# Moving three kinds of VectorE subtractions to GpSimd, with a new order of plain and Winograd chunks, in a one-core encoder layer

## Chip, cores, metric

The kernel runs on one core of one Trainium2 chip. The metric is the device time of one execution in microseconds. Before the change three executions took 937.6, 938.48 and 938.74 us, so the median is 938.48 us.

## What is computed

One layer of a streaming encoder for 512 tokens of width 1024, in float32:

```
x = x + 0.5 * swiglu_ffn(rms_norm(x, ffn1_norm), ffn1_w_in, ffn1_w_out)
h = rms_norm(x, mix_norm); q, k, v, xr, gate = split(h @ w_in_proj)
x = x + concat([diff_attention(q, k, v, ...), rg_lru_branch(xr, gate, ...)]) @ w_out_proj
x = x + 0.5 * swiglu_ffn(rms_norm(x, ffn2_norm), ffn2_w_in, ffn2_w_out)

def swiglu_ffn(h, w_in, w_out):          # w_in: 1024 x 5632, w_out: 2816 x 1024
    g, u = split(h @ w_in)
    return (silu(g) * u) @ w_out
```

The change touches the two feed-forward blocks (FFN 1 and FFN 2).

## The kernel before

**Arithmetic.** Each float32 operand of a large matmul is split into a high part in fp32r (`w_hi`, `t_hi`, `act_hi`, made by ScalarE with a Copy that rounds) and a low part (`w_lo`, `t_lo`, `act_lo`, the difference, made by VectorE). A product is three matmuls, high by high, high by low and low by high (lines 1367 to 1369 in `product`). Everything is held transposed: features on the 128 partitions, 512 tokens along the free dimension.

**Chunks.** The work of an FFN is a list of chunks, one weight load of 640 to 1024 KB each, into two slots by parity (`raw`, `w_hi`, `w_lo`). The 22 tiles of the hidden dimension stand in two groups of 10 and 12. Each group's input chunks are followed by 8 output chunks ("O"). The first 4 input chunks of an FFN are plain ("P"): 8 steps of contraction for the gate and 8 for the up part, 512 columns wide, 48 matmuls. The others, 6 in the first group and 12 in the second, are Winograd-Strassen chunks ("W"): seven block products instead of eight, each of 4 steps, 3 matmuls and 256 columns, so 84 matmuls. The products are called op 0 to op 6.

**Operands of a W chunk.** For the moving side, x is combined once per FFN from blocks of pairs of feature tiles into T1 to T4 (`t_bases` on ScalarE, `t_made_of` on VectorE, T1 being a plain difference of two halves of x, line 864) and then split (`t_highs`, `t_lows`). For the weights, VectorE makes four sums per chunk (`s123`, `s4`), ScalarE rounds them (`s_highs`), VectorE takes their low parts (`s_lows`). The low parts of the unsummed blocks come from ScalarE writing minus the high part (`minus_highs`, line 521) and a GpSimd DMA that adds `raw` to it (`a_lows`, line 463).

**Results of a W chunk.** Op 0 gives Q6 and op 1 gives Q1. ScalarE copies both out of PSUM (`copies(c, 0)`, `copies(c, 1)`, line 544); op 3 accumulates into the bank that held Q6 and waits for the first copy. VectorE forms Q1 - Q6 (`take_q6`, line 911), Q5 (`take_q5`), the two halves of the up part (`up_earlier`, `up_later`) and of the gate (`gate_later`, `gate_earlier`, the latter ending in line 943); ScalarE applies silu (line 549); VectorE multiplies (`product`, line 959); ScalarE rounds the result (`act_highs`, line 554), VectorE takes its low part (`act_lows`, line 965).

**Order.** Nothing is scheduled automatically. Each engine's queue is written out by hand per chunk (`plain_step`, `wino_step`, `out_step`), and semaphores hold an instruction until what it needs is there. An engine executes its queue in order, so a waiting instruction holds all behind it. In ScalarE's `wino_step(c)` the order is: `minus_highs(c+1)`, `act_highs(c-1)`, `copies(c, 0)`, `s_highs(c+1, 0)`, `copies(c, 1)`, `a_highs(c+1)`, the other `s_highs(c+1)`, `silu(c)`. In the plain chunks PSUM banks alternate between two sets, so TensorE waits before chunk k (k of 2 and 3) for `prod_made` of chunk k-2. At the end of the squares VectorE computes the reciprocal of the root (`reciprocal_root`, line 848), and only then, in `plain_step`, the first T blocks and the first gate.

Of the kernel before, what the change touches and what calls it, by code (L numbers as in the profile page):

```python
# [28 lines left out]
F32 = mybir.dt.float32  # L29
# [7 lines left out]
P = 128  # L37
# [98 lines left out]
def build(nc, xT, pos, cols_in, rows_in, bd_in, w_in1, w_out1a, w_out1b, w_rnn, w_qkv, w_proj, w_in2, w_out2a, w_out2b, out):  # L136
    stack = ExitStack()
    with stack:
# [14 lines left out]
        rows = sb("rows", [P, 6 * MAP_DIM])  # L153
# [16 lines left out]
        x = region("x", [P, KT * SEQ], F32, tile_at(0))  # L170
        raw = region("raw", [P, 2 * SLOT], F32, tile_at(8))

        w_hi = region("w_hi", [P, 2 * SLOT], F32R, tile_at(16))
        ws_hi = region("ws_hi", [P, 2 * BLOCK], F32R, tile_at(24))
        ws_lo = region("ws_lo", [P, 2 * BLOCK], F32R, tile_at(26))
        w_lo = region("w_lo", [P, 2 * SLOT], F32R, tile_at(28))

        t_hi = region("t_hi", [P, 2 * KT * SEQ], F32R, tile_at(36))
        t_lo = region("t_lo", [P, 2 * KT * SEQ], F32R, tile_at(52))
        h_hi = region("h_hi", [P, KT * SEQ], F32R, tile_at(36))  # L180
        h_lo = region("h_lo", [P, KT * SEQ], F32R, tile_at(44))
        base = tile_at(52)
        act_at = 68
        act_hi = region("act_hi", [P, GROUP[1] * SEQ], F32R, tile_at(act_at))
        act_lo = [region(f"act_lo{g}", [P, GROUP[g] * SEQ], F32R, tile_at(act_at + (14, 12)[g])) for g in range(2)]
        pairbuf = [region(f"pairbuf{b}", [P, 4 * SEQ], F32, tile_at(act_at + (10, 6)[b])) for b in range(2)]
        sums = region("sums", [P, 4 * BLOCK], F32, tile_at(92))
        up_s = region("up_s", [P, 2 * SEQ], F32, tile_at(96))
        assert tile_at(98) <= nc.sbuf_usable_end, (tile_at(98), nc.sbuf_usable_end)
# [3 lines left out]
        at = base  # L193
        places = {}
        for name, size in (("gt", 4 * KB2), ("xc", 4 * KB2), ("ra", 4 * KB2), ("ib", 4 * KB2),
                           ("th", 4 * KB2), ("qn", 4 * KB2), ("kn", 4 * KB2), ("v", 4 * KB2), ("qT", 4 * KB2),
                           ("kT", 4 * KB2), ("a", 2 * KB2), ("aT", 2 * KB2), ("bd", 2 * KB2)):
            places[name] = at
            at += size
        assert at <= tile_at(98)  # L200
        at = tile_at(24)
        for name, size in (("xrp", 2 * XP * 4), ("mask", (P + 64) * 4), ("st", 128 * 4), ("decay", 2 * RT * 4),
                           ("map_gain", 8), ("eps_o", 4)):
            places[name] = at
            at += -(-size // 32) * 32
        assert at <= tile_at(28)
# [17 lines left out]
        map_gain = region("map_gain", [P, 2], F32, places["map_gain"])  # L224
        eps_o = region("eps_o", [P, 1], F32, places["eps_o"])
# [40 lines left out]
        op_done, copied, post, t_made = sem("op_done"), sem("copied"), sem("post"), sem("t_made")  # L266
        t_base, t_step, t_sums, t_high, t_low = (sem(n) for n in ("t_base", "t_step", "t_sums", "t_high", "t_low"))
# [42 lines left out]

        def s_place(op, s):
# [18 lines left out]
        q_parts = [[region(f"q_part{m}{n}", [P, HALF], F32, tile_at((36, 52)[m]) + n * 4 * KB2) for n in range(4)] for m in range(2)]  # L330
# [24 lines left out]

        def half(t, c, n):
            return t[:, c % 2 * SEQ + n * HALF:c % 2 * SEQ + (n + 1) * HALF]
# [17 lines left out]

        T_SUMS = ((0, 1), (2, 3), (), ())
        T_SPLIT = ((), (0, 1), (2, 3), ())
# [6 lines left out]
        def _(sp):  # L384
# [23 lines left out]
            def load_ffn(f, first):  # L408
                c = C_FFN[f]
                w_in, w_outs = ((w_in1, (w_out1a, w_out1b)), (w_in2, (w_out2a, w_out2b)))[f]  # L410
                for g in range(2):
# [3 lines left out]
                    for d in range(KT):  # L415
                        load(w_outs[g], d, c + OUT_AT[g] + d, OUT_COLS[g])
# [9 lines left out]
            sp.dma_start(rows[:, :], rows_in).then_inc(params_landed[1], 16)  # L426
# [16 lines left out]
        def _(pool):  # L443
# [21 lines left out]

            def ffn(f):
                for c in range(C_FFN[f], C_FFN[f] + FFN_CHUNKS):
                    if kind(c) == "W":
                        a_lows(c)
# [16 lines left out]
        def _(act):  # L486
# [82 lines left out]
            def plain_step(f, c):  # L569
                following = kind(c + 1)  # L570
                k = c - C_FFN[f]
                if following == "P" and k >= 2:
                    highs(c + 1, IN_COLS)
                if following == "W":
                    minus_highs(c + 1)
                    s_highs(c + 1, 0, c - 1)
                    a_highs(c + 1)
                    s_highs(c + 1, 2)
                    s_highs(c + 1, 3)
                for p in T_SPLIT[k]:  # L580
                    t_highs(f, p)
                for p in T_SUMS[k]:
                    t_bases(f, p)
                silu(f, c)
                if following == "W":
                    s_highs(c + 1, 5, c)
                act_highs(f, c)

            def wino_step(f, c):
                following = kind(c + 1)  # L590
                if following == "W":
# [9 lines left out]
                if following == "W":  # L601
# [7 lines left out]
            def out_step(f, c):  # L609
# [15 lines left out]
                if (f, g) == (0, 0) and d == 5:  # L625
# [11 lines left out]
            def ffn(f):  # L637
# [11 lines left out]
                if f == 0:  # L649
                    squares(EARLY_SQUARES, KT)  # L650
                    act.wait_ge(consts_made, CONSTS_FIRST)
                if kind(c0 + 2) == "P":
                    highs(c0 + 2, IN_COLS)
                root((1, 3)[f])
# [161 lines left out]
        def _(dve):  # L816
# [29 lines left out]
            def reciprocal_root(n):  # L846
# [3 lines left out]
                dve.memset(sq_sum[:, :], 0.0).then_inc(dve_step, 1)  # L850
                links[0] += 1
                dve.wait_ge(rstd_made, n)
                dve.wait_ge(dve_step, links[0])

            LATER, EARLIER = slice(HALF, SEQ), slice(0, HALF)

            def t_made_of(f, p):
# [3 lines left out]
                steps = 2 * (KT // 2 * f + p)  # L861
                if p >= 2:
                    dve.wait_ge(t_low, KT // 2 * f + p - 1)
                dve.tensor_tensor(t_block(p, T1), even[:, LATER], even[:, EARLIER], ALU.subtract).then_inc(t_step, 1)
                dve.wait_ge(t_base, KT // 2 * f + p + 1)
                dve.scalar_tensor_tensor(t_block(p, T3), even[:, EARLIER], g_even, t_block(p, B22), ALU.mult, ALU.subtract)
                dve.wait_ge(t_step, steps + 1)
                dve.scalar_tensor_tensor(t_block(p, T2), t_block(p, T1), g_even, t_block(p, B22), ALU.mult, ALU.add).then_inc(t_step, 1)
                dve.wait_ge(t_step, steps + 2)
# [36 lines left out]
            def take_q6(c):  # L906
                w = wino_of(c)
                dve.wait_ge(copied, 2 * w + 2)
                if w >= 2:
                    dve.wait_ge(post, 5 * w - 6)  # L910
                dve.tensor_tensor(q16(c), q1_copy(c), q6_copy(c), ALU.subtract).then_inc(t_made, 1)

            def take_q5(c):
                w = wino_of(c)
# [34 lines left out]
            def product(f, c):  # L949
# [4 lines left out]
                else:  # L954
# [3 lines left out]
                    up = bank[3 * (c % 2) + 1][:, :]  # L958
                dve.tensor_tensor(both(up_s, c), up, both(gate_s, c), ALU.mult).then_inc(prod_made, 1)  # L959

            def act_lows(f, c):
                n = tile_of(c - C_FFN[f])
                g = int(n >= GROUP[0])
                dve.wait_ge(act_high, FT * f + n + 1)
                dve.tensor_tensor(tile(act_lo[g], n - FIRST_TILE[g]), both(up_s, c), tile(act_hi, n - FIRST_TILE[g]).bitcast(F32),
                                  ALU.subtract).then_inc(act_low, 1)

            def plain_step(f, c):
                k = c - C_FFN[f]
                following = kind(c + 1)  # L970
                if following == "P" and k >= 2:
# [753 lines left out]
```

## Time and profile before

| | value |
|---|---|
| median of 3 runs | 938.48 us |
| profiled execution, its own time | 937.22 us |
| its span, first to last instruction | 935.4 us |
| mean granted TensorE clock | 0.996 |
| busy: TensorE matmul / weight load | 97% / 85% of the span |
| busy: VectorE / ScalarE / GpSimd | 72% / 51% / 4% |
| DMA | 117.69 MB, 126 GB/s on average |

A busy TensorE is not TensorE at its peak: matmuls are pipelined, so one that is shown as 0.28 us long starts 0.12 us after the one before it. The pace is read from the starts. The profile also gives, in brackets, how long an engine was idle ahead of an instruction and what released it.

### The profile page before, as it was taken

The page shows a single profiled execution, that of the slowest core. Times are in us where ns is not written, and L with a number is a line of the kernel's source. Part 1 is how long each engine was busy: PE and PEld are TensorE (multiplying, and loading weights), DVE is VectorE, ACT ScalarE, POOL GpSimd, SP SyncE. Part 2 cuts the span into 40 slices and gives each one's busy share as a digit, 9 for nine tenths or more (in the row PEclk, how much of TensorE's full clock was granted, in tenths as well). Part 3 has the DMA queues.
Part 4 walks back from the last instruction along what each step waited for, and adds up shares of the span by engine and source line. Part 5 has one row for each costly group of instructions (what it writes and reads, how often), then busy time and mean ns, then how long its engine had stood idle before and what let it go on. Part 6 is the DMA issues. An engine that isn't in the chain of part 4 may idle for free.

```text
span 935.4 us, 14482 instructions
## 1 busy us (share of the span) xinstructions
PE 905.8 (97%) x5450; PEld 797.3 (85%) x5450; DVE 669.1 (72%) x1196; ACT 474.6 (51%) x803; POOL 34.1 (4%) x61
## 2 busy tenths in 40 slices
PE   8889999999999999999997999989999999999998
PEld 7679988899999888777885778779988899999886
DVE  6878865688887575765879777778854688887442
ACT  7466622465664333356647654466622465665220
POOL 0000000000000000000000000000000000010000
PEclk9999999999999999999999999999999999999999
DMA  7147522566664234222221021247532676664340
GB/s 268 57 133 184 155 99 87 176 181 174 185 174 122 98 101 141 106 91 90 90 91 46 1 91 51 85 128 186 148 108 84 179 182 164 195 170 124 122 134 34
DMA packets 21500, 117.69 MB, mean 126 GB/s; under 512 B 2640, under 2 KB 2768, under 8 KB 14160
## 3 DMA queue, kind: packets, MB, share of 16 engines
q1 hardware_dynamic: 16128, 88.32, 27.1%
q0 software_dynamic: 5328, 28.84, 15.5%
q8 instruction: 21, 0.34, 0.1%
q14 instruction: 23, 0.19, 0.1%
HBM read 86.74 MB, written 2.10 MB: 95 GB/s over the span
## 4 chain that ended last, share of the span: by engine, by line
PE 53%; DVE 18%; ACT 16%; issue 11%; DMA 1%; SPq 0%; DVEq 0%; ACTq 0%
PE bank L1367 17%; PE bank L1369 16%; PE bank L1368 16%; ACT w_lo L521 4%; ACT w_hi L527 3%; DVE sums L892 3%; DVE ws_lo L904 2%; ACT ws_hi L538 2%; ACT act_hi L554 2%; ACT q_part L544 2%; DVE sq L943 1%; DVE up_s L929 1%; DVE sq L941 1%; DVE sq L935 1%; DVE w_lo L831 1%
## 5 line engine op out<-in xcount | busy, mean ns | idle before, releaser
L1367 PE MATMUL bank<-t_hi,w_hi 128*128 128x256 f32 (+1 forms) x848 | 256.7, 303 | 10.6 <-DVE up_s L959 5.4
L1368 PE MATMUL bank<-t_lo,w_hi 128*128 128x256 f32 (+1 forms) x848 | 254.7, 300 | 0.0
L1369 PE MATMUL bank<-t_hi,w_lo 128*128 128x256 f32 (+1 forms) x848 | 254.7, 300 | 0.0
L1367 PEld LDWEIGHTS bank<-t_hi,w_hi 128*128 128x128 f32 x848 | 163.0, 192 | 18.6 <-issue 7.8
L1368 PEld LDWEIGHTS bank<-t_lo,w_hi 128*128 128x128 f32 x848 | 163.2, 192 | 5.7 <-issue 0.5
L1369 PEld LDWEIGHTS bank<-t_hi,w_lo 128*128 128x128 f32 x848 | 163.0, 192 | 5.4
L501 ACT ACTIVATE w_hi<-raw 128x1024 fp32r<-128x1024 f32 (+2 forms) x106 | 89.0, 887 | 146.2 <-PE bank L1369 146.2
L1367 PE MATMUL bank<-act_hi,w_hi 128*128 128x512 f32 x352 | 137.0, 389 | 0.0
L1368 PE MATMUL bank<-act_lo,w_hi 128*128 128x512 f32 x352 | 137.0, 389 | 0.0
L1369 PE MATMUL bank<-act_hi,w_lo 128*128 128x512 f32 x352 | 136.9, 389 | 0.0
L831 DVE TENSOR_TENSOR w_lo<-raw,w_hi 128x1024 fp32r<-128x1024 f32 (+2 forms) x106 | 103.5, 1018 | 14.6 <-ACT w_hi L501 14.0
L1035 DVE SCALAR_TENSOR_TENSOR up_s<-bank,rstd 128x512 f32<-128x512 f32 x32 | 22.1, 690 | 103.9 <-PE bank L1369 103.9
L1367 PE MATMUL bank<-t_hi,ws_hi 128*128 128x256 f32 x288 | 84.4, 293 | 5.0 <-ACT q_part L544 3.5
L549 ACT ACTIVATE sq<-sq 128x512 f32<-128x512 f32 x44 | 27.8, 632 | 119.4 <-DVE sq L943 88.4
L1368 PE MATMUL bank<-t_lo,ws_hi 128*128 128x256 f32 x288 | 81.4, 283 | 0.0
L1369 PE MATMUL bank<-t_hi,ws_lo 128*128 128x256 f32 x288 | 81.3, 282 | 0.0
L1369 PEld LDWEIGHTS bank<-act_hi,w_lo 128*128 128x128 f32 x352 | 66.1, 188 | 13.8
L1367 PEld LDWEIGHTS bank<-act_hi,w_hi 128*128 128x128 f32 x352 | 66.1, 188 | 13.7
L1368 PEld LDWEIGHTS bank<-act_lo,w_hi 128*128 128x128 f32 x352 | 66.1, 188 | 13.4
L538 ACT ACTIVATE w_hi<-sums 128x512 fp32r<-128x512 f32 x72 | 45.1, 627 | 56.1 <-PE bank L1369 45.6
L904 DVE TENSOR_TENSOR w_lo<-sums,w_hi 128x512 fp32r<-128x512 f32 x72 | 49.6, 688 | 31.1 <-ACT w_hi L538 31.1
L1367 PEld LDWEIGHTS bank<-t_hi,ws_hi 128*128 128x128 f32 x288 | 55.0, 191 | 10.9 <-ACT q_part L544 7.1
(216 smaller groups left out, 1532.4 us busy)
## 6 DMA issues: line engine op xcount, KB each, us to landing
raw<-w_in_dram SPq DMA_DIRECT2D x43, 1024.0 KB, 4.8
w_lo<-raw POOLq DMA_DIRECT2D x36, 768.0 KB, 5.7
raw<-w_out1b_dram SPq DMA_DIRECT2D x8, 768.0 KB, 4.3
raw<-w_qkv_dram SPq DMA_DIRECT2D x6, 1024.0 KB, 4.8
raw<-w_out2b_dram SPq DMA_DIRECT2D x8, 768.0 KB, 4.4
raw<-w_out1a_dram SPq DMA_DIRECT2D x8, 640.0 KB, 3.8
raw<-w_out2a_dram SPq DMA_DIRECT2D x8, 640.0 KB, 3.8
raw<-w_rnn_dram SPq DMA_DIRECT2D x4, 1024.0 KB, 4.8
```

What stands on the lines that cost most here:

```text
L501: act.activation(w_hi[:, part], raw[:, part], ACT.Copy).then_inc(high_made, 1)
L521: act.activation(w_lo[:, at:at + A_COLS], raw[:, at:at + A_COLS], ACT.Copy, scale=-1.0).then_inc(minus_made, 1)
L527: act.activation(w_hi[:, part], raw[:, part], ACT.Copy).then_inc(high_made, 1)
L538: act.activation(hi[:, at:at + BLOCK], s_sum(op), ACT.Copy).then_inc(s_high, 1)
L549: act.activation(both(gate_s, c), both(gate_s, c), ACT.Silu).then_inc(silu_made, 1)
L831: dve.tensor_tensor(w_lo[:, part], raw[:, part], w_hi[:, part].bitcast(F32), ALU.subtract).then_inc(low_made, 1)
L892: dve.tensor_tensor(s_sum(0), s_sum(2), raw_block(c, 0), ALU.add).then_inc(s2_made, 1)
L904: dve.tensor_tensor(lo, s_sum(op), hi.bitcast(F32), ALU.subtract).then_inc(s_low, 1)
L1035: dve.scalar_tensor_tensor(both(up_s, c), bank[OUT_BANK + s][:, :], 0.5, rstd[:, :], ALU.mult, ALU.mult).then_inc(y_taken, 1)
L1367: pe.matmul(dst, s_hi, m_hi, start=first, stop=False, skip_group_check=added)
L1368: pe.matmul(dst, s_hi, m_lo, start=False, stop=False, skip_group_check=added)
L1369: return pe.matmul(dst, s_lo, m_hi, start=False, stop=last, skip_group_check=added)
```

## The change

1. A new map of SBUF. The weights come first, then the region of activations, then t_lo, t_hi, x and raw. The last four, and the `q_part` buffers in them, are shifted by 64 bytes (`T_SHIFT`). `rows` moves into a region that the summed weights use, so its load and what reads it come later (second output group of FFN 1).
2. GpSimd now makes T1 (`t_ones`), Q1 - Q6 (`take_q6`) and the low parts of the activations (`act_lows`). They stand in its queue with the DMA of `a_lows`.
3. In ScalarE's `wino_step(c)`: `copies(c, 0)`, `minus_highs(c+1)`, `copies(c, 1)`, `act_highs(c-1)`, `s_highs(c+1, 0)`, `a_highs(c+1)`, the other `s_highs`, `silu(c)`. In VectorE's, `s_lows(c+1, 0)` comes after `take_q5`, and `s_lows(c+1, 2)` and `(c+1, 3)` both come after `up_earlier`.
4. The four plain chunks have four pairs of PSUM banks, and TensorE no longer waits for `prod_made` between them. The first two T blocks are made before or around the reciprocal root, the weights of the fourth plain chunk are split a chunk earlier, and the sum of squares of FFN 2 is taken inside the first plain chunk.

```diff
-        T_SUMS = ((0, 1), (2, 3), (), ())
-        T_SPLIT = ((), (0, 1), (2, 3), ())
+        ACT_AT, T_LO_AT, T_HI_AT, X_AT, RAW_AT, T_SHIFT = 20, 50, 66, 82, 90, 64
+        t_lo = region("t_lo", [P, 2 * KT * SEQ], F32R, tile_at(T_LO_AT) + T_SHIFT)
+        t_hi = region("t_hi", [P, 2 * KT * SEQ], F32R, tile_at(T_HI_AT) + T_SHIFT)
+        PLAIN_BANKS = ((0, 1), (3, 4), (2, 7), (5, 6))
...
+            # GpSimd
+            def t_ones(f, p):
+                if f == 0:
+                    pool.wait_ge(x_landed[2 * p], 16)
+                else:
+                    pool.wait_ge(x_updated, X_UPDATED[1] + 2 * p + 1)
+                if p >= 2:
+                    pool.wait_ge(t_low, KT // 2 * f + p - 1)
+                even = tile(x, 2 * p)
+                pool.tensor_tensor(t_block(p, T1), even[:, LATER], even[:, EARLIER], ALU.subtract).then_inc(t_one, 1)
+            def take_q6(c):
+                w = wino_of(c)
+                pool.wait_ge(copied, 2 * w + 2)
+                if w >= 2:
+                    pool.wait_ge(post, 5 * w - 6)
+                pool.tensor_tensor(q16(c), q1_copy(c), q6_copy(c), ALU.subtract).then_inc(t_made, 1)
+            def act_lows(f, c):
+                n = tile_of(c - C_FFN[f])
+                g = int(n >= GROUP[0])
+                pool.wait_ge(act_high, FT * f + n + 1)
+                pool.tensor_tensor(tile(act_lo[g], n - FIRST_TILE[g]), both(up_s, c), tile(act_hi, n - FIRST_TILE[g]).bitcast(F32),
+                                   ALU.subtract).then_inc(act_low, 1)
+            def wino_step(f, c):
+                if kind(c + 1) == "W":
+                    a_lows(c + 1)
+                take_q6(c)
+                if kind(c - 1) != "O":
+                    act_lows(f, c - 1)
+                if kind(c + 1) == "O":
+                    act_lows(f, c)
...
             # ScalarE
             def wino_step(f, c):
                 following = kind(c + 1)
+                copies(c, 0)
                 if following == "W":
                     minus_highs(c + 1)
                 else:
                     highs(c + 1, OUT_COLS[c - C_FFN[f] >= IN_AT[1]])
-                if kind(c - 1) == "W":
+                copies(c, 1)
+                if kind(c - 1) != "O":
                     act_highs(f, c - 1)
-                copies(c, 0)
                 if following == "W":
                     s_highs(c + 1, 0)
-                copies(c, 1)
-                if following == "W":
                     a_highs(c + 1)
...
             # VectorE
             def wino_step(f, c):
                 following = kind(c + 1)
                 if following == "W":
                     s4(c + 1)
-                    s_lows(c + 1, 0)
-                if kind(c - 1) == "W":
-                    act_lows(f, c - 1)
-                take_q6(c)
                 take_q5(c)
                 if following == "W":
-                    s_lows(c + 1, 2)
+                    s_lows(c + 1, 0)
                 up_earlier(c)
                 if following == "W":
+                    s_lows(c + 1, 2)
                     s_lows(c + 1, 3)
...
+            def plain_step(f, c):
+                if k == 0:
+                    gate(f, c)
+                    t_lows(f, 0)
+                    product(f, c)
+                    t_lows(f, 1)
+                    lows(c + 3, IN_COLS)
+                if k == 1:
+                    gate(f, c)
+                    t_made_of(f, 2)
+                    product(f, c)
+                    t_made_of(f, 3)
+                    s123(first_wino)
+                if k == 2:
+                    gate(f, c)
+                    t_lows(f, 2)
+                    product(f, c)
+                    t_lows(f, 3)
+                    s4(first_wino)
+                    s_lows(first_wino, 0)
+                    s_lows(first_wino, 2)
+                    s_lows(first_wino, 3)
+                if k == 3:
+                    gate(f, c)
+                    product(f, c)
+                    s_lows(first_wino, 5)
+                    s123(first_wino + 1)
...
             # TensorE
             def plain(f, c, meanwhile=None):
-                k = c - C_FFN[f]
                 pe.wait_ge(low_made, lows_through(c))
-                if k >= 2:
-                    pe.wait_ge(prod_made, FT * f + k - 1)
```

## Rows read from the trace of the kernel before

**Rows 1.** The page, busy time of each engine over the span.
```profile
PE 905.8 (97%) x5450; PEld 797.3 (85%) x5450; DVE 669.1 (72%) x1196; ACT 474.6 (51%) x803; POOL 34.1 (4%) x61
```
**Rows 2.** Waits of TensorE: us in total, times, longest.
```profile
PE bank L1367 <- DVE up_s L959: 5.4, 2, 4.2
PE bank L1367 <- DVE w_lo L831: 4.5, 3, 2.5
PE bank L1367 <- ACT q_part L544: 3.5, 4, 1.8
```
**Rows 3.** Timeline of TensorE in W chunks: start, duration, line, operands.
```profile
215.50 0.39 PE L1367 MATMUL bank<-t_hi,ws_hi 128*128 128x256 f32 x1
...
224.24 0.28 PE L1367 MATMUL bank<-t_hi,ws_hi 128*128 128x256 f32 x1
...
225.56 0.28 PE L1369 MATMUL bank<-t_hi,ws_lo 128*128 128x256 f32 x1
225.89 0.38 PE L1367 MATMUL bank<-t_hi,ws_hi 128*128 128x256 f32 x1
```
**Rows 4.** Timeline of TensorE, third and fourth plain chunk of FFN 2.
```profile
598.11 0.47 PE L1367 MATMUL bank<-t_hi,w_hi 128*128 128x512 f32 x1 [1.19 <-DVE up_s L959]
...
608.88 0.39 PE L1369 MATMUL bank<-t_hi,w_lo 128*128 128x512 f32 x1
611.76 0.50 PE L1367 MATMUL bank<-t_hi,w_hi 128*128 128x512 f32 x1 [2.49 <-DVE w_lo L831]
```
**Rows 5.** Stretches after stalls: length, busy by engine, PEclk, DMA.
```profile
36.20:38.90 2.70, 2.70 (x6) 2.12 (x7) 1.70 (x3) 2.70 (x5) 0.00 (x0) 0.50 0.00 0
...
611.80:616.00 4.20, 4.20 (x12) 3.29 (x13) 3.50 (x6) 1.36 (x2) 0.00 (x0) 0.59 0.74 250
```
**Rows 6.** Timeline of ScalarE over one W chunk.
```profile
223.04 0.63 ACT L549 ACTIVATE sq<-sq 128x512 f32<-128x512 f32 x1 [2.23 <-DVE sq L943]
223.58 1.47 ACT L521 ACTIVATE w_lo<-raw 128x1536 fp32r<-128x1536 f32 x1
224.96 0.61 ACT L554 ACTIVATE act_hi<-up_s 128x512 fp32r<-128x512 f32 x1
225.48 0.36 ACT L544 ACTIVATE q_part<-bank 128x256 f32<-128x256 f32 x1
225.74 0.62 ACT L538 ACTIVATE w_hi<-sums 128x512 fp32r<-128x512 f32 x1
...
233.44 0.63 ACT L549 ACTIVATE sq<-sq 128x512 f32<-128x512 f32 x1 [2.24 <-DVE sq L943]
```
**Rows 7.** Timeline of VectorE, same chunk.
```profile
228.66 0.69 DVE L904 TENSOR_TENSOR ws_lo<-sums,ws_hi 128x512 fp32r<-128x512 f32 x1 [0.30 <-ACT ws_hi L538]
229.26 0.42 DVE L929 TENSOR_TENSOR up_s<-bank,q_part 128x256 f32<-128x256 f32 x1
229.60 0.68 DVE L904 TENSOR_TENSOR ws_lo<-sums,ws_hi 128x512 fp32r<-128x512 f32 x1
```
**Rows 8.** Timeline of GpSimd, same chunk.
```profile
225.35 0.86 POOL L463 DMA_DIRECT2D w_lo<-raw  x1 [9.53 <-ACT w_lo L521]
```
**Rows 9.** Groups by form on GpSimd: busy us, mean ns, idle before.
```profile
L452 POOL MEMSET sq_sum<- 128x512 f32 x1 | 0.5, 526 | 0.0
```
**Rows 10.** Groups by form on VectorE: the two moved in W chunks.
```profile
L965 DVE TENSOR_TENSOR act_lo<-up_s,act_hi 128x512 fp32r<-128x512 f32 x44 | 30.2, 687 | 10.6 <-ACT act_hi L554 10.4
L911 DVE TENSOR_TENSOR q_part<-q_part,q_part 128x256 f32<-128x256 f32 x36 | 15.1, 419 | 2.0 <-ACT q_part L544 2.0
```
**Rows 11.** Timeline, all engines, ahead of FFN 1's third plain chunk.
```profile
22.66 1.99 ACT L501 ACTIVATE w_hi<-raw 128x1024 fp32r<-128x1024 f32 x2
23.73 2.36 DVE L831 TENSOR_TENSOR w_lo<-raw,w_hi 128x1024 fp32r<-128x1024 f32 x2
...
26.69 3.35 DVE L848 RECIPROCAL rstd<-rstd 128x512 f32<-128x512 f32 x1 [0.59 <-ACT rstd L513]
```
**Rows 12.** The page, DMA issues: KB each, median us to landing.
```profile
w_lo<-raw POOLq DMA_DIRECT2D x36, 768.0 KB, 5.7
```

More of the change, by code:

```diff
@@ new lines, in build @@
+        act_hi = region("act_hi", [P, GROUP[1] * SEQ], F32R, tile_at(ACT_AT))
+        act_lo = [region(f"act_lo{g}", [P, GROUP[g] * SEQ], F32R, tile_at(ACT_AT + (14, 12)[g])) for g in range(2)]
+        pairbuf = [region(f"pairbuf{b}", [P, 4 * SEQ], F32, tile_at(ACT_AT + (10, 6)[b])) for b in range(2)]
+        sums = region("sums", [P, 4 * BLOCK], F32, tile_at(ACT_AT + 24))
+        up_s = region("up_s", [P, 2 * SEQ], F32, tile_at(ACT_AT + 28))
+        t_lo = region("t_lo", [P, 2 * KT * SEQ], F32R, tile_at(T_LO_AT) + T_SHIFT)
@@ L569, in plain_step @@
             def plain_step(f, c):
-                following = kind(c + 1)
                 k = c - C_FFN[f]
-                if following == "P" and k >= 2:
-                    highs(c + 1, IN_COLS)
-                if following == "W":
[L575 to L587, printed above, removed]
+                first_wino = C_FFN[f] + PLAIN[f]
+                if k == 0:
+                    for p in (0, 1):
+                        t_highs(f, p)
+                    highs(c + 3, IN_COLS)
+                    silu(f, c)
+                    t_bases(f, 2)
+                    act_highs(f, c)
+                    t_bases(f, 3)
+                if k == 1:
+                    silu(f, c)
+                    t_highs(f, 2)
+                    act_highs(f, c)
+                    minus_highs(first_wino)
+                    t_highs(f, 3)
+                if k == 2:
+                    silu(f, c)
+                    s_highs(first_wino, 0, c)
+                    act_highs(f, c)
+                    s_highs(first_wino, 2)
+                    s_highs(first_wino, 3)
+                    a_highs(first_wino)
+                if k == 3:
+                    silu(f, c)
+                    s_highs(first_wino, 5, c)
             def wino_step(f, c):
                 following = kind(c + 1)
+                copies(c, 0)
                 if following == "W":
@@ L957, in product, with gate @@
                         dve.wait_ge(act_low, FT * f + c - C_FFN[f] - 1)
-                    up = bank[3 * (c % 2) + 1][:, :]
+                    up = plain_bank(f, c, 1)
                 dve.tensor_tensor(both(up_s, c), up, both(gate_s, c), ALU.mult).then_inc(prod_made, 1)
[L961 to L968, printed above, removed]
-                k = c - C_FFN[f]
-                following = kind(c + 1)
-                if following == "P" and k >= 2:
-                    lows(c + 1, IN_COLS)
-                for p in T_SPLIT[k]:
-                    t_lows(f, p)
-                for p in T_SUMS[k]:
-                    t_made_of(f, p)
-                if following == "W":
-                    s4(c + 1)
-                    for op in S_OPS[:3]:
-                        s_lows(c + 1, op)
-                    s123(c + 2)
+            def gate(f, c):
+                k = c - C_FFN[f]
                 dve.wait_ge(g_done, (0, PLAIN[0])[f] + k + 1)
@@ L1385, in h_parts, with in_tile @@
                 return h_tile(t_hi, k), h_tile(t_lo, k)
[L1387 removed]
+            def in_tile(f, c, g, ks=range(KT)):
                 for k in ks:
[L1390 removed]
+                    mm = product(plain_bank(f, c, g), weights(c % 2, (2 * k + g) * P), h_parts(k), k == 0, k == KT - 1)
                     if k == KT - 1:
```

165 lines of the change are left out of this document (92 added, 73 removed).

## Prediction

> **What bounds the kernel now.** I read the page first. TensorE shows a matmul in 97% of the span [rows 1], so only time in which it starts matmuls late or slowly can be won. The view of waits lists what it waited for: two waits for a product in the plain chunks (5.4 us), three for low parts of weights (4.5 us), four for the copies of Q (3.5 us) [rows 2]. These are only the waits that show as idle. The timeline shows the shorter ones. Inside a product, matmuls start every 0.12 us: twelve of them, counted from 224.24, end with the one that starts at 225.56. The next should start at 225.68 and starts at 225.89, and it holds up its successor by another 0.1 us [rows 3]. The same place was passed at 215.50, so a chunk takes 10.39 us, while 84 x 0.12 is 10.07 (the pace averages 0.1199). That loss of 0.32 us stands at op 3 of 25 of the 36 W chunks. Five others lose more (2.0, 1.2, 0.7, 0.6 and 0.2 us; the four long waits for the copies are in these), six nothing. Together 25 x 0.32 + 4.7 = 12.7 us.
>
> What sets 10.39 is seen on the other engines. ScalarE starts silu at 223.04 and 233.44, and between the two its only long idle time is at the end, waiting for line 943 of VectorE [rows 6]. VectorE's run from the low part at 228.66 on is in its turn released by ScalarE's rounding [rows 7]. So there is a ring: silu, minus, act_highs, copy, rounding, on to the s_high of op 2, which is 5.62 us from silu to 228.66; then s_lows, up_earlier, s_lows, s123 and the gate, 4.78 us, to the next silu. Sum 10.40. TensorE's stall is the difference to its 10.07, and the copy is where the ring holds it.
>
> **Plain chunks.** Here the stalls cost twice. After the 4.2 us wait the granted clock is 0.50 of full speed for 2.7 us, and after the 2.5 us wait 0.59 for 4.2 us [rows 5]: 1.35 and 1.72 us lost.
>
> *FFN 1.* TensorE's third plain chunk needed the product of the first, which came late because the reciprocal (3.35 us), the clearing of the sum and two T pairs stood ahead of it. With four pairs of banks this wait is gone, and its next one is for the weights of that chunk. They are split by about 26.1 (23.73 + 2.36) [rows 11], 6 us before TensorE asks. Weights of the fourth plain chunk: ScalarE can round them when the second chunk is done (about 32) and is through at 34; then silu with its table load, product about 36.7, a T split, and the two halves by VectorE (2.36) until about 40.2. TensorE wants them at 42.9. Gone are 4.17 + 1.17 idle, 0.16 more at each restart, 1.35 of clock and 0.15 of slow first matmuls: 7.15 us.
>
> *FFN 2.* Same steps: 1.19 and 2.49 idle [rows 4], 0.16 twice, 1.72 of clock: 5.7 us. A plain chunk has 10.77 us between first and last start [rows 4], and VectorE's list for it (gate, two T items, product, weights or sums) comes to 6 to 8 us, so it gains 2 to 3 us on TensorE per chunk; that is the cover for everything moved here. The sum of squares only changes place. The moved T1s run on an idle GpSimd. The late low parts at the start of the first W chunk of FFN 1 (0.7 us) go too, as `minus` is issued some 10 us ahead of need and lands in 5.7 us [rows 12].
>
> **W chunks.** The new ScalarE order has the same instructions, so silu to s_high of op 2 stays 5.62. On VectorE `up_earlier` leaves the stretch behind it: 229.60 - 229.26 = 0.34 [rows 7]. The ring becomes 10.40 - 0.34 = 10.06, a tie with TensorE's 10.07. act_lows and take_q6 (mean 687 and 419 ns, starts 0.60 and 0.34 apart) [rows 10] stood in VectorE's pause before the ring's part and were no term of it; their going only widens the pause. The second effect is slack. The copy of Q6 now starts 0.54 after silu, where it was 2.44 (225.48 - 223.04) [rows 6]. TensorE goes on 0.41 after it starts, and needs this at 3 x 1.44 = 4.32 after its chunk began, so silu may be 3.37 late instead of 1.47; now it is 1.7 late, and at each group's start I get 1.4 to 1.5. There are 1.9 us in reserve per group.
>
> So without any effect between engines all 12.7 us go. Sum: 7.15 + 5.7 + 0.7 + 12.7 = 26.2, and the profiled execution's own 937.2 becomes 911.0. The median lies 1.3 above it: 912.3.
>
> **What GpSimd's work costs.** No row shows a two-input operation there. Its memset of 512 columns takes 526 ns [rows 9]; that, one write per element, is the lower bound, and three such passes (two reads and a write), 1.6 us, the upper. I take the middle, 1.1 us, and 0.6 for 256 columns. Its queue, from silu: the DMA issue starts 1.77 after `minus` [rows 6, 8], now at 2.58, until 3.44; Q1 - Q6 until 4.04; act_low until 5.14. That is all, 2.6 us in 10 with the DMA, and its readers come later (the gate at 9.2). By itself it hides.
>
> The open cost is whether VectorE is held meanwhile. The only row with both busy, the DMA issue at 225.35, shows no lengthening of VectorE's instructions, so the lower bound is zero. Upper bound: VectorE's subtractions wait for the whole GpSimd instruction. s_low of op 0 is ready at 3.64. With 1.1 us: if VectorE gets in between, act_low ends at 5.83 and the ring grows by 0.21; if not, 5.14 + 0.60 + 0.34 = 6.08 against 5.62, 0.46. With 1.6 and 0.8: 3.44 + 0.8 + 1.6 = 5.84, + 0.94 = 6.78, 1.16. A growth d is first eaten by the reserve: the last copy of the first group comes after 4 d, of the second after 10 d, so the stall of both FFNs is 2 x ([4d - 1.97] + [10d - 1.87]), brackets not below zero. d = 0.21 gives 0.5 us, 0.46 gives 5.5, 1.16 gives 25. I take d near 0.3, 2.3 us, since it lies between the two middle cases: 914.5.
>
> The Trainium skill, page "SBUF — State Buffer", section "Who interferes with whom", has a rule that speaks against this change: a VectorE instruction with two SBUF inputs and a GpSimd instruction that reads SBUF exclude each other, and the later one is blocked until the first ends. By that rule the held cases above apply (912.8 to 937), by the row of the DMA issue the free one (912.3). The Trainium skill, page "GPSIMD Engine Reference", section 3.1, gives 4497 ns for 2048 columns of tensor_tensor there; an estimate from it is 1.1 us for 512.
>
> **Rivals.**
> - *VectorE is held hard* (d from 0.5 to 1.1, typical 0.85). For it: eight of VectorE's instructions per chunk have both inputs in SBUF. Against: GpSimd works in VectorE's pause. Stall 2 x (1.4 + 6.6) = 16: 928. Chance 0.20.
> - *It gets slower.* One mechanism: GpSimd's act_low, held or long, keeps VectorE's s_low of op 2 back in each of the 36 W chunks. It decides when d passes 1.2, where 2 x (14d - 3.84) eats the 26 us; that is an act_low of 1.65 us or more with VectorE waiting through it. At 1.5 it costs 34 us: 946. Above that bound nothing in the trace speaks for such a length. Chance 0.12.
> - *The new order doesn't do what it says.* A wait that I don't see in the plain chunks, or low parts that land late because `minus` starts 0.27 later in the ring (its reserve at op 1 is about 2 us with 5.7 to land [rows 12]), gives half the gain back: 925 to 936. Chance 0.10.
> - *The shift changes the pace.* 0.1199 us per 256 columns is 13 ns more than 256 cycles of 2.4 GHz, and 0.2275 for 512 is 14 ns more. It is the same for all operands, wherever they lie, which speaks for a fixed cost; but all of them start on multiples of 512 bytes, so no row excludes alignment. 2 ns on the some 3400 matmuls with t operands would be 7 us, all of it 44. Below 906 with a chance of 0.08.
>
> **Numbers.** Forecast 914.5 (its own range 909 to 919) with a chance of 0.50. Below 906: 0.08; above 936: 0.12; the rest, 920 to 936, 0.30. The range 906 to 936 holds 0.8. A measurement of this kernel can tell 0.2% (1.9 us) from no change. Faster is the forecast, the hard-held case, the alignment case and most of the third rival: 0.84. Same 0.03, slower 0.13.
>
> **What would show it.** Right: no wait of TensorE for a product or for weights in the plain chunks but the first (0.8 us, before 20 us), clock at full after 36 us; W chunks 10.07 us apart, at least in each first group; GpSimd's two-input operations near 1.1 and 0.6 us. If VectorE is held, its s_lows of op 0 are longer than 0.69 us or start late after their rounding, and copies of Q6 hold TensorE only late in the groups of 12. Wrong: longer matmul pace, waits for `w_lo` landing, or stalls from the first W chunk of a group on.

## The result and the profile after

The changed kernel takes 929.7 us (median of 4 runs, 929.01 to 930.15) against 938.08 us for the kernel before (4 runs, 937.6 to 938.74). The ratio is 0.991, with a 95% interval of 0.9892 to 0.9927. The gain of 8.4 us is real, but the forecast was 914.5 us, which is 23.6 us below the kernel before. The profiled execution has a span of 927.0 us.

The page, busy time by engine, answers to [rows 1]:

```profile
PE 896.0 (97%) x5450; PEld 788.7 (85%) x5450; DVE 685.5 (74%) x1107; ACT 470.9 (51%) x802; POOL 132.8 (14%) x149
```

VectorE has 89 instructions fewer and is 16 us busier. That is the first sign: some of the instructions that are left have become longer. TensorE's waits, as in [rows 2]:

```profile
PE bank L1440 <- DVE up_s L991: 14.1, 24, 0.7
PE bank L1440 <- DVE q_part L980: 3.2, 2, 1.7
...
PE bank L1440 <- DVE w_lo L903: 0.6, 1, 0.6
```

The waits for a product and all but one for low parts of weights are gone. A new one has come: 24 times TensorE waits for `up_earlier` (line 991). (Two waits for a weight DMA, 0.57 and 0.24 us before, have become one of 0.15.) The plain chunks are clean. These windows hold the stretches in which the stalls and the low clock stood (the columns are those of [rows 5]), with TensorE busy throughout and the clock at full:

```profile
31.00:39.00 8.00, 8.00 (x37) 6.56 (x36) 6.01 (x8) 5.47 (x7) 2.28 (x2) 1.00 0.00 0
597.00:620.00 23.00, 23.00 (x130) 20.03 (x130) 22.20 (x31) 14.79 (x24) 12.01 (x8) 1.00 0.46 134
```

One W chunk. ScalarE, to be read beside [rows 6]:

```profile
215.80 0.63 ACT L606 ACTIVATE sq<-sq 128x512 f32<-128x512 f32 x1 [4.12 <-DVE sq L1005]
...
226.53 0.63 ACT L606 ACTIVATE sq<-sq 128x512 f32<-128x512 f32 x1 [4.13 <-DVE sq L1005]
```

From silu to silu it is 10.73 us, where it was 10.40 and was to become 10.06. GpSimd in this chunk:

```profile
229.11 0.88 POOL L471 DMA_DIRECT2D w_lo<-raw  x1 [7.83 <-ACT w_lo L578]
229.72 1.04 POOL L490 TENSOR_TENSOR q_part<-q_part,q_part 128x256 f32<-128x256 f32 x1
230.43 1.58 POOL L496 TENSOR_TENSOR act_lo<-up_s,act_hi 128x512 fp32r<-128x512 f32 x1
```

VectorE in this chunk:

```profile
229.12 0.42 DVE L980 TENSOR_TENSOR q_part<-bank,q_part 128x256 f32<-128x256 f32 x1 [0.28 <-ACT q_part L601]
230.16 2.41 DVE L972 TENSOR_TENSOR w_lo<-sums,w_hi 128x512 fp32r<-128x512 f32 x1 [0.61 <-ACT w_hi L595]
232.49 0.41 DVE L991 TENSOR_TENSOR up_s<-bank,q_part 128x256 f32<-128x256 f32 x1
232.83 1.28 DVE L972 TENSOR_TENSOR ws_lo<-sums,ws_hi 128x512 fp32r<-128x512 f32 x2
```

and TensorE:

```profile
231.95 0.28 PE L1442 MATMUL bank<-t_hi,w_lo 128*128 128x256 f32 x1
232.96 0.39 PE L1440 MATMUL bank<-t_hi,w_hi 128*128 128x256 f32 x1 [0.72 <-DVE up_s L991]
```

The low part of op 0 takes 2.41 us instead of 0.69. It has two inputs in SBUF, it is ready while GpSimd is at work, and it ends at 232.57, 0.56 after GpSimd's second instruction (232.01), as if it had begun when that one ended. GpSimd ran both of its instructions in the meantime; VectorE did not get in between them. The records leave no gap there: GpSimd's second starts 0.33 us before its first ends. `up_earlier` follows, and TensorE, which wants it for op 6, starts again just after it. The effect over the whole span, groups by form on VectorE (busy us, mean ns). Before, one was 688 ns; now 28 of the 72 take about 2.41 us and the others still 0.69:

```profile
L972 DVE TENSOR_TENSOR w_lo<-sums,w_hi 128x512 fp32r<-128x512 f32 x72 | 97.7, 1356 | 16.6 <-ACT w_hi L595 16.6
```

At the first W chunk of each first group another instruction is caught. VectorE's `s4`, 0.69 us long when free, takes 2.75, until 0.55 us after GpSimd's end (59.83 + 1.56 = 61.39), and TensorE waits 1.7 and 1.45 us for `take_q5` behind it:

```profile
59.19 2.75 DVE L967 TENSOR_TENSOR sums<-sums,raw 128x512 f32<-128x512 f32 x1
61.87 0.41 DVE L980 TENSOR_TENSOR q_part<-bank,q_part 128x256 f32<-128x256 f32 x1
```

### The profile page after: what moved, and what is told of

It reads as the page before. It is cut to its first block, busy times and chain, and to the rows that moved or that the text cites. A ratio compares the mean times of both kernels' runs of the same rounds, so it can differ in the third digit from the quotient of the medians.

```text
span 927.0 us, 14491 instructions
## 1 busy us (share of the span) xinstructions
PE 896.0 (97%) x5450; PEld 788.7 (85%) x5450; DVE 685.5 (74%) x1107; ACT 470.9 (51%) x802; POOL 132.8 (14%) x149
## 4 chain that ended last, share of the span: by engine, by line
PE 63%; issue 14%; DVE 13%; ACT 9%; DMA 1%; SPq 0%; DVEq 0%; ACTq 0%
PE bank L1440 20%; PE bank L1442 20%; PE bank L1441 20%; DVE ws_lo L972 3%; ACT w_lo L578 2%; DVE sums L960 2%; ACT q_part L601 2%; ACT w_hi L595 2%; ACT act_hi L611 1%; DVE up_s L991 1%; DVE sq L1005 1%; PE bank L1681 1%; DVE sq L1003 1%; DVE sq L997 1%; PE bank L1658 1%
## 5 line engine op out<-in xcount | busy, mean ns | idle before, releaser
L1442 PE MATMUL bank<-t_hi,w_lo 128*128 128x256 f32 (+1 forms) x848 | 251.2, 296 | 0.0
L1441 PE MATMUL bank<-t_lo,w_hi 128*128 128x256 f32 (+1 forms) x848 | 250.8, 296 | 0.0
L1440 PEld LDWEIGHTS bank<-t_hi,w_hi 128*128 128x128 f32 x848 | 159.2, 188 | 30.7 <-DVE up_s L991 19.4
L1441 PEld LDWEIGHTS bank<-t_lo,w_hi 128*128 128x128 f32 x848 | 159.2, 188 | 5.9 <-issue 0.5
L1442 PEld LDWEIGHTS bank<-t_hi,w_lo 128*128 128x128 f32 x848 | 159.2, 188 | 5.0
L903 DVE TENSOR_TENSOR w_lo<-raw,w_hi 128x1024 fp32r<-128x1024 f32 (+2 forms) x106 | 108.9, 1068 | 16.3 <-ACT w_hi L558 16.0
L972 DVE TENSOR_TENSOR w_lo<-sums,w_hi 128x512 fp32r<-128x512 f32 x72 | 97.7, 1356 | 16.6 <-ACT w_hi L595 16.6
L496 POOL TENSOR_TENSOR act_lo<-up_s,act_hi 128x512 fp32r<-128x512 f32 x44 | 73.0, 1660 | 52.0 <-ACT act_hi L611 52.0
L1440 PE MATMUL bank<-t_hi,ws_hi 128*128 128x256 f32 x288 | 80.3, 279 | 0.0
L471 POOL DMA_DIRECT2D w_lo<-raw x36 | 31.6, 878 | 336.5 <-ACT w_lo L578 336.5
```

The lines of the kernel that those rows point to most:

```text
L471: pool.dma_start(w_lo[:, at:at + A_COLS].bitcast(F32), raw[:, at:at + A_COLS], accum_op=ALU.add).then_inc(low_landed[c % 2], 16)
L496: pool.tensor_tensor(tile(act_lo[g], n - FIRST_TILE[g]), both(up_s, c), tile(act_hi, n - FIRST_TILE[g]).bitcast(F32), ALU.subtract).then_i ...
L903: dve.tensor_tensor(w_lo[:, part], raw[:, part], w_hi[:, part].bitcast(F32), ALU.subtract).then_inc(low_made, 1)
L972: dve.tensor_tensor(lo, s_sum(op), hi.bitcast(F32), ALU.subtract).then_inc(s_low, 1)
L1440: pe.matmul(dst, s_hi, m_hi, start=first, stop=False, skip_group_check=added)
L1441: pe.matmul(dst, s_hi, m_lo, start=False, stop=False, skip_group_check=added)
```

## Experiments

Theory A after the result: GpSimd's instructions hold VectorE's. Theory B: the new order is itself too late. Each experiment changes the changed kernel or the first experiment, only the twelfth the kernel before. Times are medians, with the lowest and highest run in brackets.

**1. Everything back on VectorE** (map, shift and order kept).

```diff
@@ GpSimd, wino_step @@
-                take_q6(c)
-                if kind(c - 1) != "O":
-                    act_lows(f, c - 1)
-                if kind(c + 1) == "O":
-                    act_lows(f, c)
...
@@ VectorE, where the T blocks are made @@
+                dve.tensor_tensor(t_block(p, T1), even[:, LATER], even[:, EARLIER], ALU.subtract).then_inc(t_one, 1)
...
@@ VectorE, wino_step @@
                 take_q5(c)
+                take_q6(c)
+                if kind(c - 1) != "O":
+                    act_lows(f, c - 1)
                 if following == "W":
                     s_lows(c + 1, 0)
```

> The changed kernel with T1, Q1 - Q6 and the low parts of the activations back on VectorE (in its pause: after take_q5 come take_q6, act_lows, then the low part for op 0). Map, 64-byte shift and new order stay. Theory A (GpSimd's two-input instructions hold VectorE's, and that is what lengthened the ring from 10.06 to 10.73 us per W chunk): the low part for op 0 falls from about 2.4 us to 0.69, W chunks stand 9.85 to 10.1 us apart, TensorE's waits for up_earlier (14 us) are gone, time 903 to 912. Theory B (the new order itself puts up_earlier too late for op 6, whoever makes the differences; VectorE with more work is no better): W chunks stay above 10.4 us, time 925 or more.

Measured: 907.52 us (906.51 to 908.68), ratio 0.9678 (0.9662 to 0.9694). TensorE's wait for `up_earlier` is gone and silu to silu is 10.06 us:

```profile
219.75 0.63 ACT L594 ACTIVATE sq<-sq 128x512 f32<-128x512 f32 x1 [2.81 <-DVE sq L1008]
...
229.81 0.63 ACT L594 ACTIVATE sq<-sq 128x512 f32<-128x512 f32 x1 [2.98 <-DVE sq L1008]
```

Theory B falls. Moving work *to* GpSimd, alone, costs 22 us. Four short waits of TensorE for the DMA of `w_lo` (0.16 to 0.38 us) have come in its place.

**2. The same without the shift.** `T_SHIFT = 0`.

> As the kernel with all three back on VectorE, and T_SHIFT 0 in place of 64. In the changed kernel matmuls of W chunks start 0.117 us apart where they started 0.120 apart before. If the shift makes this pace: 0.120 again, 84 of them 10.07 us, and the time 2 to 8 us above the kernel with the shift (8 us where TensorE is the bound in all 36 W chunks, little where the ring at about 10.06 is). If the new places of the regions make it, or anything else: 0.117 stays and the two times agree within 1 us.

Measured: 912.17 us (911.07 to 912.85). The shift does change the pace. The first matmul on `ws_hi`, in successive W chunks, without the shift, is 10.08 apart:

```profile
211.37 0.28 PE L1451 MATMUL bank<-t_hi,ws_hi 128*128 128x256 f32 x1
...
221.45 0.28 PE L1451 MATMUL bank<-t_hi,ws_hi 128*128 128x256 f32 x1
```

With it the distance is 9.89 in nearly all chunks in which TensorE doesn't wait, and in a few of FFN 2 it is less, down to 9.52.

**3 and 4. One kind alone on VectorE:** `act_lows` (Q1 - Q6 and T1 stay on GpSimd), or `take_q6` (`act_lows` and T1 stay).

> The changed kernel with only the low parts of the activations back on VectorE; T1 and Q1 - Q6 stay on GpSimd (1.0 us recorded, about 0.7 apart). Theory A: GpSimd's Q1 - Q6 runs from 3.2 to 3.9 us after silu; the low part of the activation and the one for op 0 follow it on VectorE and end by 5.2, before the ring needs VectorE at 5.6. Time within 3 us of the kernel with all on VectorE. Theory B: above 925.

> The changed kernel with only Q1 - Q6 back on VectorE; the low parts of the activations and T1 stay on GpSimd. Theory A: GpSimd's act_low (1.59 us) starts at about 3.2 to 3.5 us after silu, before VectorE's low part for op 0 is ready (3.6), and holds it to about 5.0; up_earlier and the low part for op 2 follow at 5.6 and 5.9, where the ring wants 5.6: W chunks 10.1 to 10.4 us apart, time 910 to 920, between the other two. Theory B: as the changed kernel, 927 to 930.

Measured: 908.28 us (907.4 to 909.47) and 909.93 us (909.33 to 911.09); the fourth is just faster than expected. Each alone costs 0.8 or 2.4 us, both together 22 (the 0.8 lies within the spread of the runs, and T1, which stays on GpSimd in both, is in it). In experiment 3 Q1 - Q6 holds VectorE's `act_lows` (1.69 us instead of 0.69) and silu to silu is 10.09. In experiment 4 VectorE is held too,

```profile
214.79 1.72 DVE L971 TENSOR_TENSOR w_lo<-sums,w_hi 128x512 fp32r<-128x512 f32 x1 [0.28 <-ACT w_hi L594]
```

but it is through at 216.51, before the next thing that the ring waits for (the rounded sums of op 2), and silu to silu stays 10.06. A hold costs time only as far as it is longer than VectorE's pause.

**5, 6 and 7. Dead work on GpSimd.** To separate being held from waiting for a result, experiment 1 gets work that nobody reads, where Q1 - Q6 and the low part stood. Here the one with two inputs, shortened: `ones_256` and `ones_512` stand for views of one constant of 128 columns, and the waits of the dead work for itself are left out. For copies it is `tensor_copy(out, ones)`, which the trace calls CAST as it writes bf16; for memsets, five of 384 columns.

```diff
+                pool.wait_ge(copied, 2 * w + 2)
+                pool.tensor_tensor(dummy_256, ones_256, ones_256, ALU.subtract)
+                pool.wait_ge(act_high, count_of(c))
+                pool.tensor_tensor(dummy_512, ones_512, ones_512, ALU.subtract)
```

> The first experiment (all three kinds of work back on VectorE, 907.5 us) with dead work on GpSimd in each W chunk, where Q1 - Q6 and the low part of the activations stood in the changed kernel: two tensor_tensor of 256 and 512 columns that read a constant twice and write a buffer that nobody reads. Nothing waits for them. Theory A, GpSimd's reading instructions hold VectorE's two-input ones: VectorE's low part of op 0 takes 2 us and more instead of 0.69, the distance of W chunks goes from 10.06 to 10.5 to 10.9 us, and the time is 918 to 935 us. Theory B, what cost the time in the changed kernel is that the results of GpSimd come late to those who wait for them: 906 to 909 us, as without the dead work.

> The same, but the dead work is five memsets of 384 columns (0.42 us each, with a wait between them about 2.5 us in all), which read nothing. Theory A (only an instruction that reads holds VectorE): VectorE's low part of op 0 stays at 0.69 us, chunks 10.06, time 906 to 909.5 us. Theory C, any busy GpSimd holds or slows VectorE: chunks 10.5 and more and 918 to 935 us, like the dead work with two inputs.

> The same, but the dead work is two tensor_copy of 256 and 512 columns, with one input each. Theory A: VectorE's two-input instructions that become ready meanwhile start when the copy ends; the copies are shorter than the tensor_tensor (0.3 to 0.8 us each I think), so the ring grows by 0 to 0.3 us and the time is 907 to 916 us; a VectorE low part of 1 us or more shows the hold. Theory D, only two-input GpSimd instructions hold: VectorE's lengths stay at 0.69 and the time at 906 to 909.5.

Measured: two inputs 937.86 us (936.56 to 938.63), ratio 0.9997 (0.9987 to 1.0007), all of the gain gone and more than the 918 to 935 us expected; memsets 908.12 us (907.46 to 908.88); copies 914.58 us (914.22 to 914.79). With two inputs, GpSimd and VectorE:

```profile
233.19 0.92 POOL L477 TENSOR_TENSOR dummy<-ones 128x256 bf16<-128x256 f32 x1
234.01 1.09 POOL L479 TENSOR_TENSOR dummy<-ones 128x512 bf16<-128x512 f32 x1
```

```profile
233.49 2.17 DVE L1002 TENSOR_TENSOR act_lo<-up_s,act_hi 128x512 fp32r<-128x512 f32 x1
235.58 0.68 DVE L981 TENSOR_TENSOR w_lo<-sums,w_hi 128x512 fp32r<-128x512 f32 x1
```

Now VectorE's own `act_lows` is caught, 2.17 us until 0.56 after GpSimd's end, and not the low part of op 0 as expected; silu to silu is 10.96. With copies (one input) it is 1.69 us long, again until 0.55 after the end of GpSimd's second, and the distance is 10.25. With memsets GpSimd is about as busy as in the changed kernel (2.4 us per W chunk for the five) and nothing is held:

```profile
223.09 0.75 POOL L477 MEMSET dummy<- 128x384 f32 x1
223.90 0.42 POOL L479 MEMSET dummy<- 128x384 f32 x1
224.44 0.42 POOL L482 MEMSET dummy<- 128x384 f32 x1
```

```profile
223.23 0.68 DVE L1009 TENSOR_TENSOR act_lo<-up_s,act_hi 128x512 fp32r<-128x512 f32 x1
223.83 0.69 DVE L988 TENSOR_TENSOR w_lo<-sums,w_hi 128x512 fp32r<-128x512 f32 x1
```

So it is reading that holds, with one input as with two, and not that GpSimd's results come late, nor that it is busy or writes. This is the rule of the Trainium skill, page "SBUF — State Buffer", section "Who interferes with whom": a VectorE instruction with two SBUF inputs contends with a GpSimd instruction that reads SBUF and not with one that only writes it, and who issues first holds the other. The traces agree that reading is what counts and that the held instruction waits to the end. On who holds whom they are less simple: VectorE's low part in the changed kernel starts 0.27 us before GpSimd's second instruction (230.16 against 230.43) and is still held behind it, and in experiment 5 VectorE's Q1 - Q6, which starts 0.27 us before GpSimd's, takes 0.65 us instead of 0.41.

**8. The same work, apart:** `act_lows` first, Q1 - Q6 after `up_earlier`.

```diff
-                take_q6(c)
                 if kind(c - 1) != "O":
                     act_lows(f, c - 1)
+                pool.wait_ge(post, 5 * wino_of(c) + 2)
+                take_q6(c)
```

> The changed kernel with the same work on GpSimd, but apart: in each W chunk the low part of the activations first, and Q1 - Q6 only after VectorE's up_earlier (a wait for post >= 5w + 2). Theory A with the two instructions back to back as the cause: the low part alone fits into VectorE's slack (as it did when only it stood on GpSimd, chunks 10.06), and Q1 - Q6 falls into VectorE's pause of 0.7 us and sticks out of it by 0.1 to 0.3 us; chunks 10.06 to 10.35, time 908 to 916 us. Rival, the amount of GpSimd work counts, wherever it stands: chunks 10.6 to 10.9, time 924 to 932 us.

Measured: 923.62 us (922.9 to 923.88), silu to silu 10.61; expected were 908 to 916 us, and 924 to 932 by the rival. By the time it lies with the rival, by the trace with neither. `act_lows` fits, as in experiment 4 (VectorE's low parts for op 2 and 3 start 5.61 us after silu here and in experiment 1). But it has eaten VectorE's pause, so Q1 - Q6 starts inside that pair of low parts, which takes 1.84 instead of 1.29 us, and these 0.55 us are the whole growth of the ring:

```profile
230.42 1.84 DVE L973 TENSOR_TENSOR ws_lo<-sums,ws_hi 128x512 fp32r<-128x512 f32 x2
```

```profile
230.58 1.13 POOL L490 TENSOR_TENSOR q_part<-q_part,q_part 128x256 f32<-128x256 f32 x1 [0.97 <-DVE up_s L992]
```

My estimate of 0.1 to 0.3 for it was too small. The amount of GpSimd work isn't the price; how it lies against VectorE's reads is.

**9, 10 and 11. Where things lie,** from experiment 1: the region of activations also shifted by 64 bytes; `T_SHIFT = 128`; `T_SHIFT = 32`.

> The first experiment (907.5 us) with act_hi, act_lo, pairbuf, sums and up_s moved 64 bytes too. If what the shift does to the 256-column matmuls of the W chunks (0.120 us from start to start without it, 0.117 with it) is a matter of where the moving matrix lies against the weights, the 1056 matmuls of 512 columns on act_hi and act_lo (0.2249 and 0.2277 us) go faster too, by up to 2.7 ns each: 904.5 to 907 us. If it comes only with 256-column matmuls, or the pace of 512 columns has another bound: within 1 us of the first experiment.

> The first experiment with T_SHIFT = 128 in place of 64. If any offset against the 2048-byte grid does it: W matmuls 0.117 us apart, 907 to 909 us. If only an offset that is odd in units of 64 bytes does it: 0.120 us again and 911.5 to 913 us, as with no shift.

> The first experiment with T_SHIFT = 32. Any offset does it: 0.117 us and 907 to 909 us; 64 bytes are needed: 0.120 us and 911.5 to 913 us.

Measured: 910.56 us (909.67 to 911.48), 912.74 us (911.68 to 913.17) and 908.46 us (907.46 to 909.02). With 128 bytes the W chunks are 10.08 us apart as with none; with 64 they take 9.89 and with 32 bytes 9.80, each in most chunks. Not in all: with 128 they take 9.97 in the first group of FFN 2, with 32 bytes 9.89 in the first group of FFN 1. Shifting the activations too was a miss, as 904.5 to 907 us were expected: the 1056 matmuls of 512 columns on `act_hi` and `act_lo` start 0.2289 us apart on average instead of 0.2268, which is some 2 of the 3 us lost. But there the first W chunks of the second groups start 9.52 us apart (168.72, 178.24, 187.76), where they take 9.89 in experiment 1, though the operands of these matmuls lie at the same places in both. So the start of the moving matrix doesn't set the pace alone; what else does is open.

**12. The kernel before with t_hi, t_lo and all behind them 64 bytes on.**

> The kernel before with t_hi, t_lo and all that lies behind them moved 64 bytes, nothing else changed. The theory is that there the ring of ScalarE and VectorE sets the distance of the W chunks (10.39 us) and TensorE waits for it: its matmuls go 0.117 us apart but the idle time grows by as much, and the time changes only where TensorE sets the pace (three first chunks of each group): 936 to 938.5 us. The rival, TensorE's pace counts wherever it works (3000 matmuls at 2.6 ns): 929 to 932 us.

Measured: 938.76 us (937.96 to 939.69), ratio 1.0008 (0.9999 to 1.0018). That is just above the 936 to 938.5 us expected and no gain. The matmuls go faster, and TensorE spends that on waiting for the copies of Q, 30 times where it showed 4 times [rows 2]:

```profile
PE bank L1368 <- ACT q_part L545: 10.9, 30, 1.1
```

**13. The changed kernel with `T_SHIFT = 0`,** to price the hold at the old pace.

> The changed kernel with T_SHIFT = 0 and nothing else. W matmuls at 0.120 us, so TensorE needs 10.08 us for a W chunk and the ring stays at 10.73. If the shift counts only where TensorE sets the pace (the first one or two chunks of each group), the time rises by 0.5 to 3 us, to 930 to 933 us, and GpSimd's work costs 18 to 21 us at the old pace (against 912.2 without it). If the pace counts in every chunk: 934 to 938.5 us.

Measured: 929.76 us (929.25 to 930.39), the same as with the shift, where a rise by 0.5 to 3 us was expected. TensorE's wait per chunk is about 0.40 us instead of 0.56 to 0.73 and silu to silu again 10.73:

```profile
232.96 0.28 PE L1442 MATMUL bank<-t_hi,w_lo 128*128 128x256 f32 x1
233.63 0.39 PE L1440 MATMUL bank<-t_hi,w_hi 128*128 128x256 f32 x1 [0.40 <-DVE up_s L991]
```

GpSimd's work costs 929.76 - 912.17 = 17.6 us at this pace (expected were 18 to 21), and it also hides the 4.7 us of the shift.

**14 and 15. The ring made shorter,** from experiment 1: ScalarE rounds the sums of ops 2 and 3 ahead of the four A blocks; then also `T_SHIFT = 32`.

```diff
-                    s_highs(c + 1, 0)
-                    a_highs(c + 1)
-                    for op in S_OPS[1:]:
+                    for op in S_OPS[:3]:
                         s_highs(c + 1, op)
+                    a_highs(c + 1)
+                    s_highs(c + 1, S_OPS[3])
```

> The first experiment (907.5 us) with ScalarE rounding the third and fourth sums (ops 2 and 3) ahead of the four A blocks (a_highs, 1.5 us) in each W chunk. The theory is a ring silu, minus, rounding of op 2, s_lows, s123, gates, silu of 10.06 us; VectorE's pause of 0.73 us ahead of the low parts of ops 2 and 3 goes, the ring becomes 9.3 to 9.5 and TensorE's 9.89 sets the distance of W chunks to the end of each group (last chunks now 10.05 to 10.5): 904.5 to 906.5 us. Rival: the A blocks come late for op 1 of the next chunk and TensorE waits for them, or the raw slot comes free later: 907.5 to 915 us.

> The same with T_SHIFT = 32, where the matmuls of a W chunk took 9.80 us against 9.89 with 64 as long as TensorE set the pace, but those of 512 columns 1 to 5 ns longer: 1 to 3 us for 36 chunks against the loss; 903.5 to 907 us, within 1.5 us of the one before.

Measured: 904.82 us (904.43 to 905.22), ratio 0.9652 (0.9636 to 0.9668), and 904.16 us (903.08 to 904.31), ratio 0.9641 (0.9625 to 0.9657), the fastest version here, by 0.7 us. In experiment 14 the same matmul of successive W chunks is 9.89 us apart to the end of each group, where in experiment 1 later distances were 10.06 and up to 10.5 (with the waits for the DMA of `w_lo`, which are gone here). Where TensorE doesn't hold it back, the ring shows its own length: 9.24 us from silu to silu in the first groups.

```profile
210.19 0.28 PE L1451 MATMUL bank<-t_hi,ws_hi 128*128 128x256 f32 x1
...
220.08 0.28 PE L1451 MATMUL bank<-t_hi,ws_hi 128*128 128x256 f32 x1
```

## Why the prediction was right and wrong

**Plain chunks and the new order: right.** The forecast without any effect between engines was 912.3 us. Experiment 2 is that kernel, with VectorE doing its own work and no shift, and takes 912.17; its span is 26.2 us shorter than that of before, the sum forecast. It isn't luck of the sum, as the parts hold too: up to the first W matmul 7.75 us are gone (forecast 7.15), from the last W matmul of FFN 1 to the first of FFN 2 5.5 (5.7), and in the W chunks 13.0 (12.7 + 0.7). In the changed kernel no FFN has a wait in its plain chunks behind the one before 20 us (0.6 us), the clock doesn't fall there, and in experiments 1 and 2 the ring is 10.06 us.

**What GpSimd's work costs: the step that failed.** Forecast was 2.3 us from "I take d near 0.3", d being what the ring grows by in each chunk; measured are 17.6, with d = 10.73 - 10.06 = 0.67. The held case in the same step had the mechanism right: the work lies from silu + 3.19 (229.72 - 226.53) to + 5.48, then the low part and `up_earlier`, and the low parts of ops 2 and 3 start at + 6.30 where experiment 1 has + 5.61. Two things put d too low. The low part of the activations takes 1.58 us, not 1.1 (Q1 - Q6 shows 1.04, but the next starts 0.71 after it, so 0.6 was fair). And VectorE doesn't get in between the two instructions. I let one row, a DMA issue beside VectorE and no operation with inputs at all, stand as a case of equal weight against the held one.

**The reserve: half right.** With d = 0.67 the formula 2 x ([4d - 1.97] + [10d - 1.87]) gives 2 x (0.71 + 4.83) = 11.1 us. In the groups of 12 it held: in experiment 13 the first three distances are 10.07 to 10.13 and the later ones 10.73, so about 1.9 us were eaten first, and both groups together take 10.2 us longer than in experiment 2, where the formula has 9.7. In the groups of 6 there was none, as the hold of `s4` in their first chunk uses it up and 1.6 us more; the later chunks then stall from the third on. They take 3.6 and 4.0 us longer than in experiment 2, 7.6 in all where the formula has 1.4. That is nearly all of the missing 6.5. The prediction had named "stalls from the first W chunk of a group on" as a sign of being wrong, and in these groups they came.

**The rivals.** "VectorE is held hard" (928 us, chance 0.20) is what happened, with d in its lower half and the loss by first chunks on top. That its 928 lies so near 929.7 is luck: it comes from a larger d (0.85) without that loss. "It gets slower" would have needed a longer hold: the dead work in experiment 5 gives d = 0.90, on top of VectorE's own act_lows, and brings the whole gain to nothing. Its bound of d = 1.2 was too high, as experiment 5 is 25.7 us above experiment 2, where the formula has 2 x (1.6 + 7.1) = 17.5 for this d. "The new order doesn't do what it says" is refuted by experiments 1 and 2; of its late low parts there are waits of 1.2 us in experiment 1 and 0.2 in experiment 2. "The shift changes the pace" was right as far as the pace does change with the layout (0.120 to 0.118 us), where I had given it 0.08; but its 7 us were the wrong kind of number. In the changed kernel the shift gives nothing (929.76 and 929.7), in the kernel before nothing that can be told, and 4.7 us only once the ring is level with TensorE.

**The stall's place.** I looked for it at op 3, where the copy of Q6 is needed. It stands at op 6, at `up_earlier`, as the hold falls between the two.

## What to carry to other kernels

An instruction is not free because its new engine is idle: ask what that engine reads while it runs, and which instruction of the old engine becomes ready in that stretch. Two GpSimd instructions that each fit into VectorE's pause (0.8 and 2.4 us) cost 22 us when they stood back to back. And a faster pace of TensorE, from a layout, was worth nothing here while the loop of the other engines was longer than TensorE's own work (10.39 and 10.73 against 9.89 us); shorten the loop first and measure the layout after.

## What the runs showed of the hardware that I had not expected

- Reading instructions of GpSimd in a row kept a waiting VectorE instruction out until the last one had ended (2.41, 2.17 and 1.69 us instead of 0.69). It goes the other way too. Behind a run of five VectorE instructions with two SBUF inputs, GpSimd's low part took 4.08 us:

```profile
51.84 4.08 POOL L496 TENSOR_TENSOR act_lo<-up_s,act_hi 128x512 fp32r<-128x512 f32 x1 [3.41 <-ACT act_hi L611]
```

- The pace of fp32r matmuls of 256 columns changes with the layout: 0.120 us with an offset of 0 or 128 bytes, 0.1178 with 64, 0.1167 with 32 in most chunks (10.08, 9.89 and 9.80 us for 84). With 64 bytes it was 0.1133 us over whole chunks (9.52 us for 84), in some of experiment 1 and in more of experiment 9, so the offset isn't the whole of it. What in the memory does this was not tested. Matmuls of 512 columns went the other way: on shifted activations 2 ns slower on average (0.2289 against 0.2268 us), and in the plain chunks 0.2333 us with 32 bytes against 0.227 with none.
- GpSimd's two-input subtraction of 512 columns took 1.56 to 1.61 us in most W chunks when it wrote fp32r from two different buffers (1.66 on average over all, the held ones included), and 1.12 us in experiment 5 when it wrote bf16 from one small buffer. Which of the two differences counts is open.
